# Fourteen one-column products dealt out among the up products of the first expert pair

## The chip, the cores and the metric

The kernel runs on one core of one Trainium2 chip. The metric is the device time of one execution in microseconds; the smaller, the better. All data are float32.

## The reference

One inference step of a small backbone for 256 tokens: 128 context tokens and 128 latent tokens, width 1024. There are four layers. The token mixer is attention, mLSTM, gated linear attention, attention; after each mixer comes a mixture of experts. The change lies in the mixture of experts, so only that is given here:

```python
scores = jax.nn.sigmoid((x @ router_w).astype(jnp.float32))
...
_, idx = lax.top_k(jnp.where(in_group, sel, -jnp.inf), TOP_K)
w = jnp.take_along_axis(scores, idx, axis=-1)
w = w / w.sum(axis=-1, keepdims=True)
combine = jnp.einsum('nk,nke->ne', w, jax.nn.one_hot(idx, N_EXPERTS, dtype=jnp.float32))
hid = jax.nn.silu(jnp.einsum('nd,edf->nef', x, wg)) * jnp.einsum('nd,edf->nef', x, wu)
y = jnp.einsum('nef,efd->nd', hid * combine[..., None].astype(hid.dtype), wd)
```

There are 16 experts, each token goes to two of them, wg and wu are 1024 x 512 and wd is 512 x 1024 for each expert.

## The kernel before

The kernel is written engine by engine, with semaphores set and awaited by hand. What stands in an engine's program in a row runs in that order. Each weight chunk is 2 MB and is loaded by SyncE's DMA queue (L463) into one of nine buffers; in a layer's expert part the order is, for each pair p of experts (p and p + 8), two chunks of wg, two of wu, two of wd. A chunk is loaded when the chunk nine places ahead of it in that order has been used: wg after the gate products ("up" is counted for them), wu after the up products, wd after the down products.

For each expert the tokens that chose it are put into up to 64 slots, and two experts share the 128 columns of a pair. The steps of a pair on TensorE (`pair`, from L1488 on) are: `up` with g = 0 (the gate products with wg, L1468), `up` with g = 1 (the up products with wu, L1468), the `scatter` of the pair before, `turn_h` (transposes of HID, L1473), `turn_w` (L1459), `turn_x` (L1445), which turns the rows that the next pair needs, and `down` (L1479). In `up`, each of the eight k steps makes one product for each of the two experts, with 64 columns of weights and 512 columns of moving data. A float32 product is two instructions in the trace, so 16 products are 32.

The rows of the first pair of a layer are gathered by products with one-hot matrices (`gather`, L1432). For the other seven pairs GpSimd reads them from the token rows in DRAM by an indirect DMA (L529). It needs the token number of each slot, in IDX. These come from TensorE: `slot_id` makes, for each of the pairs 1 to 7, two products (one for each 128 tokens) of the one-hot matrix OH, 128 columns of weights, with a single moving column of token numbers, into columns 1 to 7 of PSUM bank 3. OH is made by VectorE (L1958, semaphore "onehot"). When `slot_id` is done (semaphore "slot_id"), VectorE makes IDX from it in two small operations (L2018, L2019, semaphore "idx"), and GpSimd issues the reads for pairs 1 and 2 one after the other, and each later one when `turn_x` has used the buffer. `turn_x` for pair 1 stands inside pair 0 and waits for the first of these reads ("slot_rows1").

ScalarE's SiLU of the gate products of pair 0 waits for "slot_id" too, because its result SG lies over OH. VectorE multiplies it with the up products (HID, L1980). SG and HID of a pair are needed by `turn_h`.

Around the change, `pair` reads:

```python
for g in range(2):
    ws = [landed(pe, n0 + 6 * i + 2 * g + e) for e in range(2)]
    up(ws, here[g], "up", 2 * n + 2 if g == 0 else None)
    if first and g == 0:
        slot_id()
```

Of the kernel before, what the change touches and what calls it, by code (L numbers as in the profile page):

```python
# [34 lines left out]
NPAIR = NE // 2  # L35
# [166 lines left out]
def program(nc, I, O):  # L202

    with ExitStack() as ctx:
# [5 lines left out]
        def S(name):  # L210
            name = STEP[name][0] if name in STEP else name
            if name not in sems:
                sems[name] = ctx.enter_context(nc.semaphore(name))
            return sems[name]
# [34 lines left out]
        def ar(at, *shape):  # L249
            n = int(np.prod(shape))  # L250
            assert at + n <= ARN, (at, shape)
            return shaped(arena[:, at:at + n], shape)
# [7 lines left out]
        def c_(name):  # L260
            a, b = CONST[name]
            return CN[:, a:b]
# [4 lines left out]
        def bank(b, lo=0, hi=512):  # L267
            return PS[:, b, lo:hi]
# [21 lines left out]
        OH = ar(4096, 2, NPAIR, 2, SLOTS)  # L290
# [90 lines left out]
        def landed(pe, n):  # L381

            pe.wait_ge(S(f"landed{SLOT[n]}"), 16 * LOADS[n])
            return slot_view(CHUNKS[n][0], SLOT[n])
# [534 lines left out]
        def _(pe):  # L919
            mm, tp = pe.matmul, pe.transpose  # L920
# [18 lines left out]
            for j in range(3):  # L939
                ins = tp(bank(4, P * j, P * j + P), PT[:, j], ident)  # L940
            ins.then_inc(S("prmT"), 1)
            pe.wait_ge(S("load_x"), 32)
            for b in range(4):
                for k in (2 * b, 2 * b + 1):
                    for s in range(2):
                        ins = tp(bank(b, N2 * (k % 2) + T * s, N2 * (k % 2) + T * s + T), XR[:, s, P * k:P * k + P], ident)
# [457 lines left out]
            def moe(l):  # L1404
                n0 = POS["wg", l, 0]
                n = 2 * l + 1
                if l == 0:
                    pe.wait_ge(S("load_g"), 16 * 11)
                for k in range(KD):
                    h_ready(n, k)  # L1410
                    for s in range(2):
                        ins = mm(bank(4 + s, 0, NE), H[:, k, T * s:T * s + T], RW[:, k], start=(k == 0), stop=(k == KD - 1))  # L1412
                ins.then_inc(S("logit"), 1)
                for s in range(2):
                    for c in range(2):
                        for k in range(4 * c, 4 * c + 4):
                            ins = tp(bank(2 * s + c, P * (k % 4), P * (k % 4) + P), H[:, k, T * s:T * s + T], ident)
# [24 lines left out]
                def turn_x(banks, par, sem):  # L1442

                    for k in range(KD):
                        ins = tp(bank(banks[k // 4], P * (k % 4), P * (k % 4) + P), HT[:, par, P * k:P * k + P], ident)  # L1445
                        if k in (3, 7):
                            ins.then_inc(S(sem), 1)

                def slot_id():

                    pe.wait_ge(S("onehot"), 2 * (l + 1))
                    for p in range(1, NPAIR):
                        for s in range(2):
                            ins = mm(bank(3, p, p + 1), OH[:, s, p].rearrange("t y n -> t (y n)"), c_("tid")[:, s:s + 1], start=(s == 0), stop=(s == 1))  # L1454
                    ins.then_inc(S("slot_id"), 1)

                def turn_w(b, sem, rows=P):
                    for s in range(2):
                        ins = tp(PS[0:rows, b, T * s:T * s + T], WB[:, s].rearrange("p e t -> p (e t)")[:, 0:rows], ident)  # L1459
                    ins.then_inc(S(sem), 1)  # L1460

                def up(ws, b, sem, ready=None):

                    for k in range(KD):
                        if ready is not None and k == KD // 2:
                            pe.wait_ge(S("xg"), ready)
                        for e, w in enumerate(ws):
                            ins = mm(PS[64 * e:64 * e + 64, b, :], XG[:, k, 64 * e:64 * e + 64], w[:, k], start=(k == 0), stop=(k == KD - 1))  # L1468
                    ins.then_inc(S(sem), 1)

                def turn_h(b, sem):
                    for f in range(4):
                        ins = tp(bank(b, P * f, P * f + P), HID[:, P * f:P * f + P], ident)  # L1473
                    ins.then_inc(S(sem), 1)

                def down(ws, j, b):
                    for f in range(4):
                        for e, w in enumerate(ws):
                            ins = mm(PS[64 * e:64 * e + 64, b, :], HTS[:, f, 64 * e:64 * e + 64], w[:, f, 512 * j:512 * j + 512], start=(f == 0), stop=(f == 3))  # L1479
                    return ins  # L1480

                def scatter(par, sem, first=False, rows=P):
                    for t in range(8):
                        ins = pick(bank(t // 2, N2 * (t % 2), N2 * (t % 2) + N2), YS[0:rows, P * t:P * t + P], WTS[0:rows, par, 0:N2],
                                   first and t % 2 == 0, True)
                    ins.then_inc(S(sem), 1)

                def pair(n, par, i, first=False, more=True):  # L1488

                    here, there = BANKS[par], BANKS[1 - par]  # L1490
                    pe.wait_ge(S("xg"), 2 * n + 1)
                    for g in range(2):
                        ws = [landed(pe, n0 + 6 * i + 2 * g + e) for e in range(2)]
                        up(ws, here[g], "up", 2 * n + 2 if g == 0 else None)
                        if first and g == 0:
                            slot_id()
                    if isinstance(i, int) and i == 1:
                        pe.wait_ge(S("idx"), l + 1)
                    if not first:
                        pe.wait_ge(S("ys"), 2 * n)  # L1500
                        scatter(1 - par, "scatter", first=(i == 1))
                    pe.wait_ge(S("hid"), n + 1)
                    turn_h(here[0], "turn_h")
                    if more:
                        pe.wait_ge(S("pw"), 4 * n + (4 * l + 12))
                        turn_w(here[1], "turn_w")
                        pe.wait_ge(S(f"slot_rows{1 - par}"), 8 * i + (48 * l + 8 if par else 64 * l + 16))
                        turn_x(there, 1 - par, "gather")
                    pe.wait_ge(S("hts"), n + 1)
                    ws = [landed(pe, n0 + 6 * i + 4 + e) for e in range(2)]  # L1510
                    down(ws, 0, here[0]).then_inc(S("down"), 1)
                    if more:
                        pe.wait_ge(S("wts"), n + 2)
                    down(ws, 1, here[1]).then_inc(S("down"), 1)
# [5 lines left out]
                pe.wait_ge(S("pw"), 36 * l + 8)  # L1520
                turn_w(2, "turn_w")
                pair(q0, 0, 0, first=True)
                for i in range(1, NPAIR):
                    pair(q0 + i, i % 2, i, more=(i + 1 < NPAIR))
# [5 lines left out]
                with pe.If(nx > 0):  # L1530
                    with pe.Fori(0, nx) as i:
                        pe.wait_ge(S("back"), 32 * (l + 1))
                        pe.wait_ge(S("x_v"), x_step(before, i, "x_pw"))
                        gather((6, 7), "x_t", 64)
                        turn_w(5, "x_t", 64)
                        pe.wait_ge(S("x_v"), x_step(before, i, "x_xg"))
                        pe.wait_ge(S("x_v"), x_step(before, i, "x_wts"))
                        for j in range(2):
                            pe.wait_ge(S(f"x_landed{j}"), 16 * before + 16 * i)
                            up([slot_view("wg", SLOT[n0 + 39 + j])], 4 + j, "x_t")  # L1540
                        pe.wait_ge(S("x_v"), x_step(before, i, "x_hid"))
                        turn_h(6, "x_t")
                        pe.wait_ge(S("x_v"), x_step(before, i, "x_hts"))
                        pe.wait_ge(S("x_landed2"), 16 * before + 16 * i)
                        wd = slot_view("wd", SLOT[n0 + 41])
                        down([wd], 0, 4)
                        down([wd], 1, 5).then_inc(S("x_down"), 1)
                        pe.wait_ge(S("scatter"), q0 + 8)
                        pe.wait_ge(S("x_a"), x_step(before, i, "x_ys"))
                        scatter(0, "x_scatter", rows=64)  # L1550
# [14 lines left out]
            for c in range(2):  # L1565
                pe.wait_ge(S("h0"), KD * 2 * DEPTH + 4 * c + 4)
                for s in range(2):
                    for k in range(4 * c, 4 * c + 4):
                        ins = tp(bank(2 * s + c, P * (k % 4), P * (k % 4) + P), H[:, k, T * s:T * s + T], ident)
# [519 lines left out]
```

## Time and profile before

| | us |
|---|---|
| median of 3 runs | 1925.81 |
| the runs | 1926.28, 1918.56, 1925.81 |
| the profiled execution | 1928.63 |
| its span | 1926.8 |
| TensorE busy | 1794.3 (93% of the span) |
| VectorE busy | 478.3 (25%) |
| ScalarE busy | 387.7 (20%) |
| GpSimd busy | 40.7 (2%) |
| HBM traffic over the span | 319 GB/s |

The span is the time from the first to the last instruction of the profiled execution; 1.8 us of its time lie around it. Busy shares are averages over the whole span. In the chain of work that ended last, TensorE has 77% of the span and the DMAs 14%. In the traces, PE is TensorE's matmul, PEld its weight load, DVE VectorE, ACT ScalarE, POOL GpSimd and SP SyncE. The four expert parts begin at about 200, 800, 1258 and 1630 us; in each, the stretch that matters lies 10 to 30 us behind that.

### The profile page before, as it was taken

The numbers are of one execution on the slowest core, as the hardware profiler recorded it, in microseconds if no ns is written. First come the engines' busy times: TensorE is split into PE (matmuls) and PEld (weight loads), VectorE is DVE, ScalarE is ACT, GpSimd is POOL, SyncE is SP. The second block draws the span as 40 slices with busy tenths as digits, with TensorE's granted clock in tenths as the row PEclk, the third lists the DMA queues.
The fourth block names the chain that finished last, engine by engine and source line by source line (L and its number), as shares of the span: only waits on it lengthen the run. The fifth ranks groups of instructions, "written<-read, shape, count | busy, mean of one in ns | idle before, by whom it ended". The sixth has DMA issues, their size and how long they took to land.

```text
span 1926.8 us, 21722 instructions
## 1 busy us (share of the span) xinstructions
PE 1794.3 (93%) x8848; PEld 1060.3 (55%) x8848; DVE 478.3 (25%) x1238; ACT 387.7 (20%) x763; POOL 40.7 (2%) x52
## 2 busy tenths in 40 slices
PE   4999999989998979999989997999998999999976
PEld 2678544346636858734436565854434778444443
DVE  0243411015200341411102434231111343211102
ACT  1232200013103660200002223210001342000002
POOL 1000000000000000000000000000000000000000
PEclk8999899999999989999999998999999999999988
DMA  9977899996997232799998884489999457899960
GB/s 322 360 290 303 322 426 428 426 411 246 356 358 257 90 126 93 280 411 426 427 427 296 314 314 179 167 331 426 428 427 407 159 218 277 348 427 426 428 272 22
DMA packets 134022, 609.47 MB, mean 316 GB/s; under 512 B 12485, under 2 KB 19277, under 8 KB 108960
## 3 DMA queue, kind: packets, MB, share of 16 engines
q1 hardware_dynamic: 116880, 589.32, 76.9%
q10 hardware_dynamic: 12528, 10.70, 1.8%
q0 software_dynamic: 4512, 8.02, 1.1%
q8 instruction: 73, 1.20, 0.3%
q14 instruction: 29, 0.24, 0.0%
HBM read 606.15 MB, written 8.92 MB: 319 GB/s over the span
## 4 chain that ended last, share of the span: by engine, by line
PE 77%; DMA 14%; DVE 3%; ACT 3%; issue 2%; ACTq 1%; DVEq 0%; SPq 0%; POOLq 0%
PE PS L926 21%; PE PS L1468 18%; PE PS L1479 9%; DMA arena<-in_moe_wu 7%; PE PS L1432 6%; DMA arena<-in_moe_wg 6%; PE PS L956 4%; PE PS L1008 3%; PE PS L976 2%; PE PS L1412 1%; DMA ring<-in_w_mod 1%; PE PS L1445 1%; PE PS L994 1%; DVE RS L1606 1%; PE PS L1454 1%
## 5 line engine op out<-in xcount | busy, mean ns | idle before, releaser
L1468 PE MATMUL PS<-ring,arena 128*64 128x512 f32 x1312 | 395.7, 607 | 17.3 <-DMA arena<-in_moe_wu 9.6
L1468 PEld LDWEIGHTS PS<-ring,arena 128*64 128x64 f32 x1312 | 126.6, 140 | 213.2 <-issue 213.2
L857 ACT ACTIVATE arena<-PS 128x512 f32<-128x512 f32 (+2 forms) x131 | 71.5, 546 | 830.9 <-PE PS L1459 331.2
L1980 DVE TENSOR_TENSOR arena<-arena,PS 128x512 f32<-128x512 f32 x32 | 33.5, 1047 | 592.9 <-PE PS L1468 592.9
L926 PE MATMUL PS<-HS,ring 128*128 128x256 f32 x768 | 173.7, 384 | 4.7 <-ACT arena L716 3.0
L1468 PE MATMUL PS<-arena 128*64 128x512 f32 x576 | 173.9, 602 | 1.2 <-DMA arena<-in_moe_wg 1.2
L926 PEld LDWEIGHTS PS<-HS,ring 128*128 128x128 f32 x768 | 144.6, 191 | 31.3 <-issue 9.2
L1432 PE MATMUL PS<-arena 128*128 128x256 f32 (+3 forms) x688 | 143.8, 364 | 9.4 <-ACT arena L857 4.3
L1479 PE MATMUL PS<-ring,arena 128*64 128x512 f32 x656 | 148.8, 595 | 0.5 <-DVE arena L1961 0.5
L926 PE MATMUL PS<-arena,ring 128*128 128x256 f32 (+1 forms) x672 | 145.6, 377 | 2.3 <-ACT arena L646 1.1
L1432 PEld LDWEIGHTS PS<-arena 128*128 128x128 f32 (+1 forms) x688 | 117.6, 194 | 50.5 <-issue 22.7
L926 PEld LDWEIGHTS PS<-arena,ring 128*128 128x128 f32 x672 | 126.5, 192 | 19.6 <-ACT arena L646 1.5
L1468 PE MATMUL PS<-HS,arena 128*64 128x512 f32 x192 | 95.4, 655 | 10.8 <-DMA ring<-in_moe_wu 10.8
L926 PE MATMUL PS<-ring,HS 128*128 128x512 f32 (+1 forms) x256 | 105.0, 568 | 0.0
L956 PE MATMUL PS<-ring,CS 128*32 128x512 f32 x768 | 90.0, 608 | 8.2 <-DMA ring<-in_w_mod 6.6
L1961 DVE COPY arena<-PS 128x512 f32<-128x512 f32 (+2 forms) x100 | 68.1, 681 | 110.4 <-PE PS L1473 89.2
L1479 PEld LDWEIGHTS PS<-ring,arena 128*64 128x64 f32 x656 | 46.2, 137 | 88.2 <-issue 84.2
L1479 PE MATMUL PS<-arena 128*64 128x512 f32 x192 | 85.0, 595 | 3.4 <-DVE arena L1961 3.4
L1468 PEld LDWEIGHTS PS<-arena 128*64 128x64 f32 x576 | 55.7, 139 | 53.9 <-issue 53.9
L1479 PE MATMUL PS<-HS,arena 128*64 128x512 f32 x192 | 85.0, 595 | 0.0
L926 PEld LDWEIGHTS PS<-ring,HS 128*128 128x128 f32 x256 | 48.1, 190 | 56.1 <-issue 55.2
L1468 PEld LDWEIGHTS PS<-HS,arena 128*64 128x64 f32 x192 | 28.3, 152 | 71.5 <-issue 71.5
(328 smaller groups left out, 1709.7 us busy)
## 6 DMA issues: line engine op xcount, KB each, us to landing
ring<-in_w_mod SPq DMA_DIRECT2D x48, 2048.0 KB, 16.3
ring<-in_moe_wu SPq DMA_DIRECT2D x41, 2048.0 KB, 18.2
ring<-in_moe_wd SPq DMA_DIRECT2D x41, 2048.0 KB, 22.0
ring<-in_moe_wg SPq DMA_DIRECT2D x41, 2048.0 KB, 23.3
arena<-in_moe_wg SPq DMA_DIRECT2D x24, 2048.0 KB, 19.7
HS<-in_moe_wu SPq DMA_DIRECT2D x12, 2048.0 KB, 18.9
arena<-in_moe_wu SPq DMA_DIRECT2D x12, 2048.0 KB, 22.3
arena<-in_moe_wd SPq DMA_DIRECT2D x12, 2048.0 KB, 27.0
```

What stands on the lines that cost most here:

```text
L857: A(dst, src, func).then_inc(S(sem), 1)
L926: ins = mm(out, a, b, start=first and i == 0, stop=final and i == len(pairs) - 1)
L956: ins = mm(PS[r:r + 32, 7, :], CS[:, k, 30 - 2 * i:62 - 2 * i], w[:, k], start=(i == 0 and k < 4), stop=(i == len(MODS[g]) - 1 and k >= 4))
L976: ins = mm(bank(7, 0, N2), ones, SQ[:, k], start=(k == 0), stop=(k == KD - 1))
L994: ins = mm(bank(m, 0, N2), w[:, k, P * m:P * m + P], H[:, k], start=(k == 0), stop=(k == KD - 1))
L1008: ins = mm(bank(5 + m % 2, 0, N2), w[:, k, P * (m % 4):P * (m % 4) + P], H[:, k], start=(k == 0), stop=(k == KD - 1))
L1412: ins = mm(bank(4 + s, 0, NE), H[:, k, T * s:T * s + T], RW[:, k], start=(k == 0), stop=(k == KD - 1))
L1432: return mm(out, rows, onehot, start=first, stop=final, skip_group_check=True)
L1468: ins = mm(PS[64 * e:64 * e + 64, b, :], XG[:, k, 64 * e:64 * e + 64], w[:, k], start=(k == 0), stop=(k == KD - 1))
L1479: ins = mm(PS[64 * e:64 * e + 64, b, :], HTS[:, f, 64 * e:64 * e + 64], w[:, f, 512 * j:512 * j + 512], start=(f == 0), stop=(f == 3))
L1961: v.tensor_copy(dst, src).then_inc(S(sem), 1)
L1980: tt(by_k(HID), row(SG), row(bank(here[1])), ALU.mult).then_inc(S("hid"), 1)
```

## The change

`slot_id` no longer runs as a block between the gate products and the up products. It takes the number of a pair and makes the two products of that pair. `up` has a new argument, with which it calls `slot_id(k + 1)` behind the products of its k step, for k = 0 to 6. Only the up products (g = 1) of the first pair of each layer use it. The wait for "onehot" moves with them, ahead of the first up product. The semaphore "slot_id" is signalled by the last of the fourteen products, that is behind k = 6. The products themselves, their operands and their places in PSUM are the same, and so are the programs of the other engines.

```diff
-                def slot_id():
-
-                    pe.wait_ge(S("onehot"), 2 * (l + 1))
-                    for p in range(1, NPAIR):
-                        for s in range(2):
-                            ins = mm(bank(3, p, p + 1), OH[:, s, p].rearrange("t y n -> t (y n)"), c_("tid")[:, s:s + 1], start=(s == 0), stop=(s == 1))
-                    ins.then_inc(S("slot_id"), 1)
+                def slot_id(p):
+
+                    for s in range(2):
+                        ins = mm(bank(3, p, p + 1), OH[:, s, p].rearrange("t y n -> t (y n)"), c_("tid")[:, s:s + 1], start=(s == 0), stop=(s == 1))
+                    if p == NPAIR - 1:
+                        ins.then_inc(S("slot_id"), 1)
...
-                def up(ws, b, sem, ready=None):
+                def up(ws, b, sem, ready=None, ids=False):
 
                     for k in range(KD):
                         if ready is not None and k == KD // 2:
                             pe.wait_ge(S("xg"), ready)
                         for e, w in enumerate(ws):
                             ins = mm(PS[64 * e:64 * e + 64, b, :], XG[:, k, 64 * e:64 * e + 64], w[:, k], start=(k == 0), stop=(k == KD - 1))
+                        if ids and k < NPAIR - 1:
+                            slot_id(k + 1)
                     ins.then_inc(S(sem), 1)
...
-                        up(ws, here[g], "up", 2 * n + 2 if g == 0 else None)
-                        if first and g == 0:
-                            slot_id()
+                        if first and g == 1:
+                            pe.wait_ge(S("onehot"), 2 * (l + 1))
+                        up(ws, here[g], "up", 2 * n + 2 if g == 0 else None, ids=(first and g == 1))
```

TensorE's program in the first pair of layer 0, before, from the last gate products on; in brackets are the semaphores awaited, landed3 and landed8 being those of the two wu chunks:

```order
L1468 MATMUL PS<-arena 64x512 [waits xg]
L1468 MATMUL PS<-arena 64x512 x7
L1454 MATMUL PS<-consts,arena 128x1 [waits onehot]
L1454 MATMUL PS<-consts,arena 128x1 x13
L1468 MATMUL PS<-HS,arena 64x512 [waits landed3,landed8]
L1468 MATMUL PS<-ring,arena 64x512
L1468 MATMUL PS<-HS,arena 64x512
L1468 MATMUL PS<-ring,arena 64x512
```

And now, in the same place (the lines are numbered one or two lower or higher, since the file has changed):

```order
L1467 MATMUL PS<-arena 64x512 [waits xg]
L1467 MATMUL PS<-arena 64x512 x7
L1467 MATMUL PS<-HS,arena 64x512 [waits onehot,landed3,landed8]
L1467 MATMUL PS<-ring,arena 64x512
L1452 MATMUL PS<-consts,arena 128x1 x2
L1467 MATMUL PS<-HS,arena 64x512
L1467 MATMUL PS<-ring,arena 64x512
L1452 MATMUL PS<-consts,arena 128x1 x2
```

The block of fourteen has become seven pieces of two, the first behind the first k step. The end of the up products of pair 0 now, and what follows on TensorE up to the down products:

```order
L1452 MATMUL PS<-consts,arena 128x1 x2
L1467 MATMUL PS<-HS,arena 64x512
L1467 MATMUL PS<-ring,arena 64x512
L1474 MATMUL PS<-consts,arena 128x128 [waits hid]
L1474 MATMUL PS<-consts,arena 128x128 x3
L1458 MATMUL PS<-consts,arena 128x128 [waits pw]
L1458 MATMUL PS<-consts,arena 128x128
L1445 MATMUL PS<-consts,arena 128x128 [waits slot_rows1]
L1445 MATMUL PS<-consts,arena 128x128 x7
L1480 MATMUL PS<-ring,arena 64x512 [waits landed5,landed4,hts]
```

The last two one-column products, which signal "slot_id", now stand one k step ahead of the end of the up products; the wait for "slot_rows1" stands where it stood.

## Rows read from the trace of the kernel before

**Rows 1.** Chain of work, layer 0: start us, us, what and how many.
```profile
205.99 7.02 PE PS L1468 x32
213.00 4.00 PE PS L1454 x28
217.01 9.57 PE PS L1468 x32
...
228.61 0.87 PE PS L1445 x8
```
**Rows 2.** Chain of work, layer 1.
```profile
813.21 3.51 PE PS L1454 x28
816.72 8.38 PE PS L1468 x32
...
827.14 0.87 PE PS L1445 x8
```
**Rows 3.** Chain of work, layer 2.
```profile
1270.56 3.49 PE PS L1454 x28
...
1275.31 9.73 DMA arena<-token_rows,IDX
...
1285.09 1.09 PE PS L1445 x8
```
**Rows 4.** Chain of work, layer 3.
```profile
1643.04 3.86 PE PS L1454 x28
1646.90 9.71 PE PS L1468 x32
...
1658.65 0.87 PE PS L1445 x8
```
**Rows 5.** Waits of TensorE, whole span: us in total, times, longest.
```profile
PE PS L1468 <- DMA ring<-in_moe_wu: 15.2, 8, 2.7
...
PE PS L1468 <- DMA arena<-in_moe_wu: 9.6, 4, 2.7
```
**Rows 6.** Windows: us, busy (instructions), PEclk, DMA share, GB/s; first row L1454 alone.
```profile
213.05:215.15 2.10, 2.10 (x20) 2.10 (x20) 1.00 0.55 133
...
217.00:222.00 5.00, 5.00 (x13) 1.41 (x14) 0.34 (x2) 1.88 (x2) 2.08 (x2) 0.50 1.00 429
...
375.40:380.00 4.60, 2.44 (x12) 1.09 (x14) 0.00 (x0) 0.10 (x1) 0.00 (x0) 1.00 1.01 431
```
**Rows 7.** Timeline of weight loads, layer 0: start, us, what, idle before.
```profile
211.55 0.14 PEld L1468 LDWEIGHTS PS<-arena 128*64 128x64 f32 x2 [0.29 <-issue]
...
212.93 0.19 PEld L1454 LDWEIGHTS PS<-consts,arena 128*128 128x128 f32 x1 [0.81 <-issue]
```
**Rows 8.** Timeline behind the block of layer 0, and HID in layer 2.
```profile
217.11 1.28 ACT L857 ACT_TABLE_LOAD   x1 [10.70 <-PE PS L1454]
...
218.34 1.07 POOL L529 DMA_INDIRECT arena<-token_rows,IDX  x1 [208.34 <-DVE IDX L2019]
218.40 0.60 ACT L857 ACTIVATE arena<-PS 128x512 f32<-128x512 f32 x1
...
1282.53 1.03 DVE L1980 TENSOR_TENSOR arena<-arena,PS 128x512 f32<-128x512 f32 x1 [8.02 <-PE PS L1468]
```
**Rows 9.** Indirect reads, us to landing: issued 218 to 219, 230 to 231, all 28.
```profile
arena<-token_rows,IDX POOLq DMA_INDIRECT x1, 8.8
...
arena<-token_rows,IDX POOLq DMA_INDIRECT x1, 9.8
...
DMA to landing us min/median/max: 7.5/10.6/12.2
```
**Rows 10.** Timeline of SP, weight loads behind the up products of layer 0.
```profile
226.96 9.90 SPq L463 DMA_DIRECT2D ring<-in_moe_wg  x2
```
**Rows 11.** Windows of 1 us in layer 0, columns as in rows 6.
```profile
226.00:227.00 1.00, 0.55 (x4) 0.00 (x0) 0.35 (x1) 0.00 (x0) 0.00 (x0) 1.00 0.12 45
...
239.00:240.00 1.00, 1.00 (x8) 0.34 (x6) 0.00 (x0) 0.00 (x0) 0.00 (x0) 1.00 0.77 246
```

## Prediction, as recorded before the result

> **What bounds the kernel now.** I read the chain of waits first, around the edited place. In layer 0 it runs through TensorE without a hole: the gate products of the first expert pair (7.02 us), the slot-number products (4.00 us from 213.00), the up products (9.57 us from 217.01). Then HID on VectorE, short transposes, the turning of the gathered rows at 228.61 (L1445), and the down products [rows 1]. So TensorE is the bound there, and each microsecond in this stretch counts. The same stretch in layers 1 and 3 looks alike [rows 2, 4]. Layer 2 is different: there the chain leaves TensorE and goes through the indirect read of token rows, 9.73 us of it, before L1445 can start at 1285.09 [rows 3]. The reader should see that this read has no slack in layer 2 and very little elsewhere. The waits say what bounds the end of each expert stage: TensorE waits for weights, 15.2 and 9.6 us over the four layers, 6.2 us a layer [rows 5]. So the weight stream ends last there, and a delay is passed on only as far as that stream is delayed too.
>
> **What goes: the block and what it does to the clock.** The up products of g = 1 took 9.57, 8.38, 8.4 and 9.71 us in the four layers (layer 2: from 1274.05, the end of its block, to 1282.45, just ahead of HID at 1282.53) [rows 1 to 4, 8]; the same 32 instructions of g = 0 took 7.02 us [rows 1]. The difference is the granted clock: 0.50 from 217 to 222 us, the lower of its two levels, right after 4 us of one-column products [rows 6]. Measured against 7.02, these stretches cost 2.55 + 1.36 + 1.38 + 2.69 = 8.0 us. The block itself took 4.00, 3.51, 3.49 and 3.86 us [rows 1 to 4]; at the full clock one of its 28 passes takes 2.10 us / 20 = 0.105 us [rows 6], or 0.11 us since passes cut by the window's edges are counted in, together 3.1 us.
>
> **What the dealt-out products cost.** The 28 passes stay: 3.1 us at the full clock. Each of the seven groups now has a change from 64-column weights to 128-column weights and back. The 16 two-expert steps of g = 0 would take 16 x 0.43 = 6.86 us at the 0.43 us by which weight loads follow each other when nothing is switched, and took 7.02; so a switch costs about 0.16 us (an estimate from [rows 1, 7]; the 0.43 is 0.14 of load and 0.29 of idle time in the first row there). Six more of them are 1.0 us. The stretch from the last gate product to the last up product becomes 7.0 + 3.1 + 1.0 = 11.1 us. It was 13.57, 11.89, 11.9 and 13.57. Gain: 2.5 + 0.8 + 0.8 + 2.5 = 6.6 us in all. Bounds: if nothing of a switch is exposed, 10.1 us a layer (4 us more gained), and 9.4 if the first load of each group hides too (7 us more); if a switch costs twice as much, 4 us less gained.
>
> Does the load of a group's first weights hide under the running product? After the gate products the first 128-column load began at 212.93 after 0.81 us of idle loader, where the 64-column loads come with 0.29 us between them [rows 7]: it did not go ahead. The Trainium skill (TensorE: Matmul & The Clock Gate, "Step-by-step: what each phase is for") says that TensorE's queue pulls a weight load ahead of running matmuls when it goes to the background weights. By that rule 7 loads of 0.1 us would hide in each layer, and the sum would be 3 us lower; the trace does not agree at this switch of shapes, and I follow the trace.
>
> Whether the clock holds: with 7.0 us of dense products in 11.1 us TensorE is more than half dense. Between 375.4 and 380 us it was busy for 2.44 of 4.6 us and the granted clock stayed 1.00 [rows 6]. I take no fall inside the stretch; a fall is a rival below.
>
> **What comes in its place: the read of the token rows.** slot_id is signalled after k = 6, one k step before the end of the up products: 0.86 + 0.16 = 1.0 us before it. Before, it was signalled ahead of all of them. Behind the signal stand, in order: VectorE's two small operations that make IDX, POOL's indirect read, L1445 on TensorE. From the end of the block (217.01) to the start of the read (218.34) 1.33 us pass [rows 1, 8], and the read then needs 8.8 us to land [rows 9]. So before, the rows were there at 227.1, 1.5 us ahead of L1445. Now the read starts at (end of up) - 1.0 + 1.33 = 0.33 us after the end of up, together with the weight loads which that end releases. A read issued in the same way, soon after weight loads (230.25), took 9.8 us; the extremes of all 28 are 7.5 and 12.2, the median 10.6 [rows 9]. I take 9.8, the row nearest in kind. L1445 then starts 10.2 us after the end of up instead of 2.04 (226.57 to 228.61): TensorE stands still for 8.1 us in each layer. Nothing on TensorE can pass it: down products, the next pair's gate products and everything else are queued behind this wait.
>
> Start of L1445 by layer: 213.00 + 11.1 + 10.2 = 234.3 (was 228.61, +5.7); 813.21 + 21.3 = 834.5 (827.14, +7.4); 1270.56 + 21.3 = 1291.9 (1285.09, +6.8); 1643.04 + 21.3 = 1664.3 (1658.65, +5.7) [rows 1 to 4]. Sum +25.6 us, gain included. Bounds by the read: 4 x (7.5 - 9.8) = -9 and 4 x (12.2 - 9.8) = +10.
>
> The Trainium skill (DMA: Bandwidth & Descriptors, "Anatomy of one DMA — SWDGE (gpsimd) path") gives about 2.0 us plus bytes over 436e3 for such a DMA alone, which for 512 KB is an estimated 3.2 us. The trace does not agree: no read landed in under 7.5 us [rows 9]. By the page's figure the sum would fall by 4 x 6.6 = 26 us to no slowdown at all; it is taken up as a rival.
>
> **SiLU.** ScalarE waits for slot_id too (SG lies over OH), then loads its table (1.28 us from 217.11) and computes for 0.60 us until 219.0, 2.0 us after slot_id [rows 8]. Now that ends 1.0 us after the end of up, so HID, transposes and turn_w come 1 us later. The wait of 8.1 us hides it: cost nothing; without that cover 1 us a layer.
>
> **The clock after the wait.** TensorE was never idle here before; now it is for about 7 us ahead of L1445 and the down products. The block before, which kept it thin for 4 us, cost 2.0 us a layer on average (8.0 / 4). I take the same 2.0, together +8; bounds 0 and 2.7 a layer.
>
> **What the weight stream gives back.** The two loads behind the first down products were issued at about 236.5, when TensorE had finished them (the SP row from 226.96 covers 9.90 us), and the stream was thin only in 239:240, at 246 GB/s [rows 10, 11]. So the earlier loads had lasted until 239, 2.5 us after the issue; less about a microsecond to get started (an estimate), 1.4 us of a delay costs the stream nothing. A delay of 8 us is beyond that, since SP has only the two loads of the end of up to issue meanwhile. With TensorE's weight waits at the end of a stage at 6.2 us, it is the stream's delay that counts: -1.4 x 4 = -5.6. Bounds: nothing back (0), or all of the waits (-24.8).
>
> **The sum.** +25.6 + 8.0 - 5.6 = +28. The profiled execution took 1928.6 us (span 1926.8 and 1.8 around it), so it becomes 1956.6. It lies 2.8 us above the median of 1925.8, on which I forecast 1954.
>
> **Rivals.**
> (A) The wait is there but is taken out of the weight waits: 25.6 + 8 = 33.6 us, less 24.8: +8.8, 1934.6. For it: the stream ends last in each stage [rows 5]. Against: the loads themselves are released by the delayed down products, and from then on the stream has no hole in which to catch up ([rows 11] show one thin microsecond).
> (B) The read comes fast, because with the later issue there are few queued bytes ahead of it. This is the case that ends on the other side. The shift of the L1445s is 4X - 13.6 us for a read of X us; at X = 3.4 us it is zero and, with a wait so short that the clock holds, the time is 1925.8; at 5.8 us it reaches +9.6. For it: the stream is nearly dry at that point (45 GB/s in 226:227) [rows 11]. Against: 7.5 us at least in 28 reads, and the two weight loads start with it.
> (C) The clock falls inside the dealt-out stretch as well: in the half of it that is dense, 7 us would take up to 14; I price it at 5 us a layer, +20 on the forecast, 1974. Against: the row at 375.4 [rows 6].
>
> **Chances and range.** Forecast 0.80, A 0.08, B 0.04, C 0.06, something else 0.02. The forecast's own range is 1941 to 1965 (read 7.5 to 12.2, clock 0 to 2.7 a layer, partly offsetting). With some of A and C the range is 1938 to 1968. Half a percent, 9.6 us, is about what a measurement of this kernel tells from no change: slower by more than that 0.89, within it 0.09 (A, most of B), faster 0.02.
>
> **What the profile of the changed kernel would show.** L1445 in the first pair of each layer waiting about 8 us for the DMA of token_rows, four times; the granted clock at 1.00 through the up products with the one-column products among them, this stretch 11.1 us long; 0.50 on the down products behind the wait; the stream's rate near zero for some microseconds ahead of the down products; SiLU's table load beginning 1 us before the end of up. I am wrong if the read lands within 4 us, if the clock is 0.50 in the dealt-out stretch, or if TensorE's weight waits nearly vanish and the stage ends where it did.

## The result and the profile after

| | before | after |
|---|---|---|
| median, us | 1924.97 (4 runs) | 1964.68 (4 runs) |
| the runs, us | 1918.56 to 1926.28 | 1958.42 to 1968.97 |
| span of the profiled execution, us | 1926.8 | 1967.2 |

The changed kernel is slower: the ratio of its time to the time before is 1.0197, with a 95% interval of 1.0166 to 1.0227 (the medians of the table alone give 1.0206). The forecast was 1954 us with a range of 1938 to 1968; the time lies in the range, 11 us above the forecast.

The chain of work of the changed kernel in layer 0, the answer to [rows 1] (start us, us, what and how many). L1467 are the gate and up products, L1452 the one-column products, L1480 the down products; L1445 has kept its number.

```profile
203.49 7.88 PE PS L1467 x36
211.36 0.54 PE PS L1452 x4
211.90 1.01 PE PS L1467 x4
...
219.62 1.01 PE PS L1467 x4
220.63 0.55 PE PS L1452 x4
...
222.50 11.20 DMA arena<-token_rows,IDX
...
233.75 1.97 PE PS L1445 x8
235.71 8.03 PE PS L1480 x32
```

The first row holds the gate products and the first k step of the up products. Then a group of one-column products and a k step follow each other, 1.55 us for both, six times. With the seventh group, at 220.63, the chain leaves TensorE and goes through the read of the token rows, as it did before in layer 2 alone [rows 3]. The same rows in layers 1, 2 and 3:

```profile
835.20 11.18 DMA arena<-token_rows,IDX
...
846.43 1.97 PE PS L1445 x8
848.39 8.89 PE PS L1480 x32
...
1301.49 11.92 DMA arena<-token_rows,IDX
...
1313.45 1.97 PE PS L1445 x8
1315.42 9.19 PE PS L1480 x32
...
1686.90 11.25 DMA arena<-token_rows,IDX
...
1698.20 1.97 PE PS L1445 x8
1700.17 7.96 PE PS L1480 x32
```

The waits of TensorE over the whole span (us in total, times, longest), to be read against [rows 5]:

```profile
PE PS L1445 <- DMA arena<-token_rows,IDX: 32.5, 4, 8.5
...
PE PS L1467 <- DMA ring<-in_moe_wu: 10.6, 5, 2.7
PE PS L1474 <- DVE arena L1981: 8.8, 4, 2.2
PE PS L1467 <- DMA arena<-in_moe_wu: 8.6, 4, 2.7
```

A new wait leads the list, once in each layer. The waits for wu have shrunk from 24.8 to 19.2 us. L1474 (turn_h) waits 2.2 us for HID, 1.0 us more than the 1.2 us it waited before: that is SiLU, which now begins late. It stands ahead of the wait for the rows and hides in it.

The clock, in windows of layer 0 (us, busy time and instructions of TensorE, its weight loads, VectorE, ScalarE, POOL, then the granted clock, the DMA share and GB/s):

```profile
212.00:222.00 10.00, 10.00 (x52) 4.34 (x50) 0.50 (x3) 0.73 (x1) 0.00 (x0) 1.00 0.93 392
...
225.20:233.70 8.50, 0.71 (x4) 0.31 (x2) 0.69 (x1) 0.38 (x1) 0.00 (x0) 0.50 1.00 419
...
233.70:237.80 4.10, 4.05 (x14) 2.34 (x16) 2.36 (x6) 0.00 (x0) 0.99 (x1) 0.51 0.32 129
```

Through the dealt-out stretch the clock stays at its upper level, where it was 0.50 behind the block [rows 6]. It falls behind it instead, at about 224.1, when TensorE had made its last up product at 222.2 and stood waiting for HID; L1445 and the first down products run at 0.50.

SP's queue and the stream of weights in layer 0, the answers to [rows 10, 11]: first the timeline, then windows.

```profile
222.22 0.33 SPq L463 DMA_DIRECT2D HS<-in_moe_wd  x1
222.59 21.52 SPq L463 DMA_DIRECT2D ring<-in_moe_wg  x2
```

```profile
236.00:244.00 8.00, 8.00 (x34) 2.44 (x32) 1.49 (x5) 0.74 (x2) 0.99 (x1) 0.89 0.11 28
```

The last row of SP covers two loads, from the issue of the first to the end of that of the second: 21.5 us, where it was 9.9. The second could be issued only at 243.8, when the down products were done. For 8 us the stream moved 28 GB/s.

### The profile page after: what moved, and what is told of

The parts are those of the page before. It is cut to its first block, busy times and chain, and to the rows that moved or that the text cites. A ratio compares the mean times of both kernels' runs of the same rounds, so it can differ in the third digit from the quotient of the medians.

```text
span 1967.2 us, 21722 instructions
## 1 busy us (share of the span) xinstructions
PE 1803.4 (92%) x8848; PEld 1060.3 (54%) x8848; DVE 478.2 (24%) x1238; ACT 386.6 (20%) x763; POOL 40.7 (2%) x52
## 4 chain that ended last, share of the span: by engine, by line
PE 78%; DMA 14%; DVE 3%; ACT 2%; issue 2%; ACTq 0%; DVEq 0%; SPq 0%; POOLq 0%
PE PS L926 22%; PE PS L1467 19%; PE PS L1480 10%; DMA arena<-in_moe_wu 6%; PE PS L1432 6%; PE PS L956 4%; DMA arena<-in_moe_wg 4%; PE PS L1008 3%; DMA arena<-token_rows,IDX 2%; PE PS L976 2%; PE PS L1445 1%; DMA ring<-in_w_mod 1%; PE PS L994 1%; PE PS L1412 1%; PE PS L1452 1%
## 5 line engine op out<-in xcount | busy, mean ns | idle before, releaser
L1467 PE MATMUL PS<-ring,arena 128*64 128x512 f32 x1312 | 392.6, 601 | 11.5 <-DMA arena<-in_moe_wu 8.6
L1467 PEld LDWEIGHTS PS<-ring,arena 128*64 128x64 f32 x1312 | 121.5, 138 | 207.3 <-issue 207.2
L1467 PE MATMUL PS<-arena 128*64 128x512 f32 x576 | 174.3, 606 | 3.4 <-DMA arena<-in_moe_wg 3.3
L1480 PE MATMUL PS<-ring,arena 128*64 128x512 f32 x656 | 154.8, 615 | 0.5 <-DVE arena L1962 0.5
L1467 PE MATMUL PS<-HS,arena 128*64 128x512 f32 x192 | 93.8, 619 | 10.2 <-DMA ring<-in_moe_wu 10.2
L1480 PEld LDWEIGHTS PS<-ring,arena 128*64 128x64 f32 x656 | 47.7, 142 | 93.4 <-issue 90.0
L1480 PE MATMUL PS<-arena 128*64 128x512 f32 x192 | 85.0, 595 | 3.4 <-DVE arena L1962 3.4
L1467 PEld LDWEIGHTS PS<-arena 128*64 128x64 f32 x576 | 55.8, 140 | 57.1 <-issue 57.1
L1480 PE MATMUL PS<-HS,arena 128*64 128x512 f32 x192 | 85.0, 595 | 0.0
L1626 DVE SCALAR_TENSOR_TENSOR X<-PS,MC,X 128x128 f32<-128x128 f32 x64 | 22.2, 346 | 177.5 <-PE PS L926 126.8
## 6 DMA issues: line engine op xcount, KB each, us to landing
ring<-in_moe_wg SPq DMA_DIRECT2D x41, 2048.0 KB, 20.6
arena<-in_moe_wg SPq DMA_DIRECT2D x24, 2048.0 KB, 19.5
arena<-in_moe_wu SPq DMA_DIRECT2D x12, 2048.0 KB, 20.5
```

The lines of the kernel that those rows point to most:

```text
L1626: stt(X[:, m, 0:T], y[:, 0:T], mod_col(l, vec, m, 0), X[:, m, 0:T], ALU.mult, ALU.add)
```

## The experiments

Times are medians; each ratio is to the kernel before, with its 95% interval. The changed kernel has 1.0197 [1.0166, 1.0227]. The kernel before was run again beside them: its median was 1925.1 us beside late_signal, dealt_early, loads_held and two_first, 1926.5 beside the other three. The ratio is not the quotient of two medians, and can differ from it by 0.2%. The traces shown are of one execution each.

| kernel | median us (runs) | ratio |
|---|---|---|
| late_signal | 1966.4 (4) | 1.0199 [1.0168, 1.0231] |
| dealt_early | 1920.6 (10) | 0.9981 [0.9955, 1.0008] |
| loads_held | 1938.3 (8) | 1.0067 [1.0040, 1.0094] |
| two_first | 1919.3 (12) | 0.9953 [0.9937, 0.9969] |
| one_sooner | 1956.9 (4) | 1.0153 [1.0112, 1.0194] |
| two_sooner | 1936.8 (10) | 1.0031 [1.0000, 1.0062] |
| filled_wait | 1953.0 (4) | 1.0115 [1.0075, 1.0155] |

### late_signal: only the signal is late

The edit is made in the kernel before, in `slot_id`, `up` and `pair`:

```diff
-                    ins.then_inc(S("slot_id"), 1)
...
+                        if late and k == KD - 2:
+                            ins.then_inc(S("slot_id"), 1)
...
+                        up(ws, here[g], "up", 2 * n + 2 if g == 0 else None, late=(first and g == 1))
```

> The block of fourteen products stays where it was before; only the signal slot_id is given one k step before the end of the up products. Theory (the late signal makes the token-row read late): the read starts 0.8 us behind the end of up and lands 11 us later, L1445 waits about 10 us in each layer, and with the lower clock behind the wait the time is about 1925 + 40 + 10 - 4 = 1971 us. Rival (dealing the products out, with its switches of weight shape, is what costs): nothing is dealt out here, only SiLU is 1 us later, so 1925 to 1930 us.

1966.4 us. The block of products is where it was; nothing is dealt out. Its chain in layer 0:

```profile
210.85 3.22 PE PS L1454 x28
214.07 7.88 PE PS L1467 x28
...
223.26 11.16 DMA arena<-token_rows,IDX
```

The late signal alone brings the whole slowdown, and the read has the same length as in the changed kernel. L1445 waits 33.7 us in all, 8.4 us a layer, where I had expected 10. The dealing out is not what costs. It also wins next to nothing against this kernel: from the first gate product to the end of up 19.0, 20.6, 19.0 and 19.0 us pass here in the four layers, and 18.8, 20.5, 18.8 and 18.8 us in the changed kernel.

### dealt_early: the products behind k = 0, 1 and 2

```diff
-                        if ids and k < NPAIR - 1:
-                            slot_id(k + 1)
+                        for p in ((1, 2, 3), (4, 5), (6, 7))[k] if ids and k < 3 else ():
+                            slot_id(p)
```

> The products are dealt out among the up products as in the changed kernel, but behind k = 0, 1 and 2 (three, two and two pairs), so the signal comes about 4 us sooner. Theory: the read starts at 14.9 us behind the first gate product and takes 8.8 to 9.7 us, as before the change, since it now runs ahead of the loads that the end of up releases; L1445 waits 3 to 4 us; about 1935 us (1930 to 1943). Rival (the switches cost): only three groups instead of seven, a gain of 4 x 4 x 0.16 = 2.6 us against the changed kernel, so about 1962 us.

1920.6 us, 14 us better than expected, and 44 us better than the changed kernel for a signal that comes 4.4 us sooner. Most of the difference to what I expected stands in the length of the first read of layer 0 (read issued between 216 and 217.5; the last number is us to landing):

```profile
arena<-token_rows,IDX POOLq DMA_INDIRECT x1, 6.5
```

I had taken 8.8 to 9.7 us from the kernel before; in the other layers it took 6.0, 6.6 and 6.1 us. L1445 waits 2.2 us in all, in two layers. The larger groups of one-column products are not free, though. In layers 2 and 3 the granted clock was at 0.50 right behind the third group (1273.3:1276.6 and 1648.8:1652.1), and the stretch up to the end of up took 19.5 us instead of 17.8 in layers 0 and 1. The row of layer 2, 20 passes that take 4.3 us at the full clock:

```profile
1273.14 6.16 PE PS L1467 x20
```

### loads_held: the weight loads wait for the read

```diff
                 for q in range(SPARE + RING, 3 * NE):
+                    if q == SPARE + RING + 2:
+                        sp.wait_ge(S("slot_rows1"), 64 * l + 16)
                     load(n + q)
```

> The changed kernel, but SyncE issues the two weight loads that the end of the first up products releases only when the first token-row read has landed. Theory (the read is long because weight loads are queued with it): with nothing queued it lands in about 3.3 us, L1445 waits less than 1 us, the stream is 2 to 4 us late in each layer against before; about 1931 us (1926 to 1940). Rival (the read has a length of its own, 9 to 11 us): L1445 still waits 8 us and the stream is held 11 us more, so 1975 us or more.

1938.3 us, and the read of layer 0 (issued between 221 and 222):

```profile
arena<-token_rows,IDX POOLq DMA_INDIRECT x1, 3.4
```

With the signal as late as in the changed kernel, and nothing else altered, the read is 3.4 us long instead of 11.2; in the other layers 4.1, 3.5 and 4.4. L1445 waits 2.3 us in all instead of 32.5. The read has no length of its own of 9 to 11 us. The median is 13 us above the kernel before. One part of that is the clock. Even without a long read TensorE waits 2.2 us for HID, since SiLU is late, and within that wait the clock falls to 0.50, at about 222.3 (L1447 is turn_x here, L1482 the down products):

```profile
224.59 1.97 PE PS L1447 x8
226.56 8.29 PE PS L1482 x32
```

This is 10.3 us where the same work took 7.9 before; over the four layers it is some 8 us more. The other likely part is the later start of the held loads, 2 to 4 us in each layer. How the 13 us divide is argued, not measured: the execution in the trace was the fastest of the eight, 1929.7 us, and shows only 1 us of them.

### one_sooner and two_sooner: the edge

One line differs from dealt_early, first in one_sooner, then in two_sooner:

```diff
+                        for p in ((1,), (2,), (3,), (4,), (5,), (6, 7))[k] if ids and k < 6 else ():
```

```diff
+                        for p in ((1, 2), (3, 4), (5,), (6,), (7,))[k] if ids and k < 5 else ():
```

> As the changed kernel, but the products of pairs 6 and 7 both stand behind k = 5, so slot_id is signalled one k step sooner, about 1.0 us. Theory (the read waits behind the weight loads that are issued ahead of it, and the end of the up products issues two): the read instruction now starts 0.7 us ahead of the end of up but writes its descriptors over 1 us, so it sits on the edge; if it gets ahead of the two loads, L1445 waits 1 to 4 us (about 1932 us), if not, it still waits about 8 us (about 1958 us). Rival (one microsecond later is one microsecond more, in proportion): 1 us less wait in each layer, 1960 us.

> As the changed kernel, but the products stand behind k = 0 to 4 (2, 2, 1, 1 and 1 pairs); the signal comes two k steps sooner, 2.3 us or so. Theory (a step, not a slope): the read starts about 2 us ahead of the end of up and ahead of the two loads, lands about 14 us behind the loads issued at the end of the gate products, at 21 to 22 us from the first gate product, and L1445 waits 1 to 2 us at most; about 1925 us (1920 to 1932). Rival (in proportion): 2.3 us less wait in each layer than in the changed kernel, 1955 us.

one_sooner: 1956.9 us, the read of layer 0 took 10.7 us and L1445 waited 30.7 us in all. That is the upper end of what I had written for the edge, 1958, and so near the rival's 1960 that this run does not decide between them. The read was issued at 220.52, 0.6 us ahead of the first of the two loads (221.10), and was as long as behind them. two_sooner: 1936.8 us, above my range of 1920 to 1932 and far below the rival's 1955; L1445 waited 18.4 us in all. Its first reads took the following times in layers 0 to 3 (us to landing):

```profile
arena<-token_rows,IDX POOLq DMA_INDIRECT x1, 10.1
...
arena<-token_rows,IDX POOLq DMA_INDIRECT x1, 7.5
...
arena<-token_rows,IDX POOLq DMA_INDIRECT x1, 9.7
...
arena<-token_rows,IDX POOLq DMA_INDIRECT x1, 4.9
```

The same program gave 4.9 us in one layer and 10.1 in another. A read signals its landing in 16 parts. In layer 0 the first landed after 2.9 us, the fifteenth after 3.6 and the last after 10.1; the read was issued at 221.01 and the two loads at 222.45 and 222.82. In layer 2 it was the same (fifteen within 4.8 us, the last after 9.7), in layer 1 two parts were late (6.9 and 7.5 us). So nearly all of each read got ahead of the loads, and L1445 waited for the one or two parts that did not. The relation is steep but not a clean step, and my two figures for two_sooner were both wrong in size.

### filled_wait: TensorE is kept busy in the wait

```diff
+                    if first:
+                        warm(17)
                     if more:
                         pe.wait_ge(S("pw"), 4 * n + (4 * l + 12))
```

> The changed kernel with 17 products of the identity (128x256, results not used) between turn_h and turn_w of the first pair, inside the wait for the read. They take about 7.5 us of a wait of 9.4. Theory (what follows the wait runs at the lower clock and loses about 2.4 us a layer): L1445 and the down products run at the full clock, 1964.7 - 9.6 = about 1955 us. Rival (the clock costs nothing here since the weight stream sets the end of the stage): 1964 us.

1953.0 us, 11.7 us less than the changed kernel; expected 9.6. The size is uncertain, since the four runs lie between 1946.0 and 1967.7 us and the trace is of the slowest, but the intervals of the two ratios do not overlap. In layer 0 the chain now reads:

```profile
225.84 10.81 DMA arena<-token_rows,IDX
...
236.69 1.10 PE PS L1445 x8
237.78 7.02 PE PS L1480 x32
```

L1445 and the down products are back at 1.10 and 7.02 us, and at 7.9 us for both together in every layer. Since the time of the whole kernel fell as well, a microsecond here is not, or not wholly, given back by the weight stream.

### two_first: what the read needs comes first

```diff
+                        ins = mm(bank(3 if p < 3 else 1, p, p + 1), OH[:, s, p].rearrange("t y n -> t (y n)"), c_("tid")[:, s:s + 1], start=(s == 0), stop=(s == 1))
+                    if p in (2, NPAIR - 1):
                         ins.then_inc(S("slot_id"), 1)
...
+                        if ids and k + 3 < NPAIR:
+                            slot_id(k + 3)
...
                             pe.wait_ge(S("onehot"), 2 * (l + 1))
+                            slot_id(1)
+                            slot_id(2)
...
+                for j, (lo, hi) in enumerate(((1, 3), (3, NPAIR))):
+                    v.wait_ge(S("slot_id"), 2 * l + j + 1)
...
+                    if p == 3:
+                        pool.wait_ge(S("idx"), 2 * l + 2)
```

> The products for pairs 1 and 2 (four of them) run as a short block ahead of the up products and are signalled at once; the other ten are dealt out behind k = 0 to 4, into PSUM bank 1, with a signal of their own. IDX is made in two parts. Theory: the first read starts 10 us behind the first gate product and lands at 19 to 20, ahead of L1445 at 20.5; no wait, the clock stays at 1.00; L1445 comes 2.0, 0.4, 1.1 and 2.0 us sooner than before, about 1920 us. Rival (the dealing costs in itself): slower than before, 1930 us or more.

1919.3 us, as expected, and below both kernels: 0.9953 of the time before. Window and chain in layer 0 (L1447 is turn_x here, L1482 the down products):

```profile
211.00:222.70 11.70, 11.70 (x62) 5.34 (x60) 2.38 (x11) 1.88 (x2) 2.08 (x2) 1.00 0.89 355
```

```profile
214.19 10.91 DMA arena<-token_rows,IDX
...
225.14 1.09 PE PS L1447 x8
226.24 7.02 PE PS L1482 x32
```

The clock is 1.00 all through, and L1447 starts 21.0 us behind the first gate product (204.18) instead of 22.5. In layers 2 and 3 it comes 0.5 and 1.8 us sooner; in layer 1 it comes 1.2 us later, because the gate products there, which had waited 3.1 us for a wg chunk, began at the lower clock and took 8.7 us instead of 7.0. L1447 waits 0.9 us in all. The read is still the last to arrive in layer 0: its 10.9 us again differ from the 8.8 I had counted with, because it starts sooner behind the loads.

## Why the prediction was right, and where its sizes were off

**The mechanism.** It is the one forecast: the signal moved behind the products that used to cover the read, and L1445 waits in every layer. late_signal shows that this alone makes the slowdown, loads_held that the wait disappears with the length of the read. The trace signs that would have refuted it are absent: the clock is 1.00 in the dealt-out stretch (rival C), and none of the four reads that L1445 waits for first was short (rival B). Rival A, the wait absorbed by the weight stream, was wrong: the waits for wu fell only from 24.8 to 19.2 us, 5.6 us, while those for wg grew from 2.8 to 4.0.

**The length of the read: taken as 9.8 us, measured 11.20, 11.18, 11.92 and 11.25.** This is the largest miss, 6 us over the four layers (45.6 instead of 39.2). I treated the length as a property of the read and chose a row that looked alike. The experiments show that it depends on what else is in the queues. In layer 0, with the second of the pair of weight loads nearest to the read as the origin:

| kernel | second load issued | read issued | length us | landed, us behind the load |
|---|---|---|---|---|
| before | 213.42 | 218.34 | 8.8 | 13.7 |
| dealt_early | 209.69 | 216.88 | 6.5 | 13.7 |
| two_first | 211.68 | 214.19 | 10.9 | 13.4 |
| changed | 222.59 | 222.50 | 11.2 | 11.1 |
| loads_held | none | 221.17 | 3.4 | |

In the first three kernels the read was issued 4.9, 7.2 and 2.5 us behind a pair of loads and landed 13.4 to 13.7 us behind it (12.8 to 14.1 over all four layers), about when the second load landed itself (13.2 to 13.5 us in layer 0). In the changed kernel it was issued together with the next pair, released by the end of the up products, and landed ahead of the second load of that pair (13.9 us). In loads_held the pair before was nearly through, with 33 GB/s in 221:222. Therefore moving the signal later cost nothing as long as the read went with the old pair, and about 8 us as soon as it went with the next one. The next pair need not be ahead of it: in one_sooner the read was issued 0.6 us sooner than the first of its loads and still took 9.7 to 11.1 us. The prediction had no place for such a step. It came near the measured value since it placed the read right, beside the loads that the end of up releases, and took the length of a read that was placed alike. The packets of the two queues in the changed kernel, in 227 to 233 us (packets, MB, share of the engines' time), show how:

```profile
q1 hardware_dynamic: 154, 2.26, 88.9%
q0 software_dynamic: 145, 0.26, 11.4%
```

and in loads_held, in 223.2 to 225 us:

```profile
q0 software_dynamic: 163, 0.29, 71.3%
```

With weights about, the small packets of the read (q0) pass one for one with large packets of the weights (q1), 145 in 6 us; alone, 163 in 1.8 us. Of the 7.8 us by which the read of layer 0 is longer than in loads_held, this has about 5; the other 2.7 pass before its first packet moves, 4.4 us behind the issue instead of 1.8, and no run shows why. The Trainium skill (DMA: Bandwidth & Descriptors, "Queues, rings and completion order") says that each DMA engine goes round its queues packet by packet; by that rule a read of few bytes but many packets pays one weight packet for each of its own, and the trace agrees (145 against 154). The fit of 2.0 us plus bytes over 436e3 (the Trainium skill, same page, "Anatomy of one DMA — SWDGE (gpsimd) path"), which I had set aside because no read was that short, gives an estimated 3.2 us; the undisturbed reads come near it, 3.4 to 4.4 us in loads_held and 3.3 us for the read at 236.49 in the changed kernel, issued into the empty stream. So I was wrong to read the trace as contradicting it: all 28 reads before were made among weight loads.

**The dealt-out stretch: forecast 11.1 us, measured 11.7** (18.76 us from the first gate product to the end of up in layers 0, 2 and 3, less 7.02). The term mis-sized is the group: 0.54 us for four passes, where 4 x 0.11 were counted; the k steps with their switch took 1.01 us, as counted (0.86 + 0.16). The first weight load of each group began after 0.81 us of idle loader, as at the one switch before:

```profile
211.29 0.52 PEld L1452 LDWEIGHTS PS<-consts,arena 128*128 128x128 f32 x4 [0.81 <-issue]
```

In layer 1 TensorE had waited for a wg chunk until 814.36, ahead of the gate products, and these ran at 0.51 of the clock for their first 3.4 us: from there to the end of up 20.45 us passed, 1.7 more. Together the stretch is 4 us longer than forecast. The wait for the chunk, 2.7 us, comes on top. It was not forecast, and not every kernel of this study had it.

**The clock behind the wait: forecast 2.0 us a layer, measured** 1.97 + 8.03 = 10.0 us for L1445 and the down products in layer 0, 10.9, 11.2 and 9.9 in the others, where before it was 7.9: 2.0 to 3.3 us, 10 in all. filled_wait confirms that it counts in the time, 11.7 us by the medians.

**The sum.** From the first gather product of a layer to that of the next the time grew by 8.1, 13.4 and 13.0 us, and by 8.4 from the last one to the end, 42.9 in all; the profiled execution had begun the first of them 2.5 us sooner, which leaves the 40.4 by which the spans differ. The forecast had 28. Counted from the same product of its layer, L1445 started 7.8, 13.9, 9.4 and 7.8 us later than before, 38.8 in all, where the forecast had 25.6: of the 13 missing the read has 6, the dealt-out stretch 4 and the wait in layer 1 3. The clock adds 10 instead of 8. Of these 49 us about 43 arrived, so some 6 were given back, where the forecast had 5.6. That this last term fits is in part luck, since it is what is left of larger sums, and executions of one kernel differ by 8 to 11 us. All the other terms came out larger than forecast and none made up for another, so that 1964.7 us lies at the very top of the forecast's own range of 1941 to 1965.

**SiLU** was costed at nothing while the wait hides it. Its 1.0 us is in the list of waits (8.8 against 4.8 us for turn_h) and was hidden, as forecast.

## What to carry to other kernels

Before work is moved behind a signal, look at what the signal starts, and not only at how long that takes but at what is queued when it is issued: here a signal 2.3 us later in layer 0 cost nothing (dealt_early) and one 6.7 us later cost 40 us (the changed kernel), depending on whether the read went with the old pair of weight loads or with the next. Give the part of a result that a long transfer waits for a signal of its own and produce it first; deal out the rest. Groups of four one-column passes among large products kept the clock up; a block of 28 did not, groups of 12, 8 and 8 did in two of four layers only, and in the idle time ahead of L1445 it fell.

## What the runs showed of the hardware that was not expected

- An indirect read of 128 rows took 3.4 to 4.4 us in loads_held with next to no weights moving, and up to 14.3 us (two_sooner) among 2 MB loads, at the same number of bytes. In the first read of each layer the first packet moved 1.6 to 1.8 us after the issue in loads_held, and 3.4 to 4.7 us after it in the kernels with weights in flight. two_sooner is an exception that no run explains: 1.6 to 1.8 us there, with weights moving at 393 GB/s in 221:222.
- The landing of such a read was tied to the loads ahead of it. In layer 0 it came 13.4 to 13.7 us behind the second load in three kernels, whether the read was issued 2.5, 4.9 or 7.2 us behind it; within each other layer the three kernels agree within 0.5 us, and over all layers it was 12.8 to 14.1 us.
- The granted clock stayed at 1.00 with four one-column passes behind each four 512-column ones for 10 us. It fell to 0.50 inside the block of 28 one-column passes before (at 215.2 in layer 0), behind the third group of dealt_early (12, 8 and 8 passes) in two of four layers, and in the changed kernel 1.5 to 3.5 us behind the last up product, ahead of the wait for the rows or early in it.
- A weight load of 128 columns did not go ahead of running 64-column products: about 0.16 us at each of seven switches, the same as at the one switch before.
